# First projections in three fp32r products, and block 0 of each feed-forward in fp32, tile by tile

## The reference, cut to what matters

```python
a  = modulate(rms_norm(h, g_mix_pre), sh1, sc1)        # ac: the same of the context
y  = mixer(a, ac)                                      # layer 0: hybrid; layer 1: conformer; then: second_block's
h  = h + gt1 * rms_norm(y, g_mix_post)
f  = swiglu_ffn(modulate(rms_norm(h, g_ffn_pre), sh2, sc2), w_ffn_in, w_ffn_out)
h  = h + gt2 * rms_norm(f, g_ffn_post)
# swiglu_ffn: gate, up = split(h @ w_in); (silu(gate) * up) @ w_out      2816 hidden
# second_block's: square(relu(h @ w_ff1)) @ w_ff2                         4096 hidden
# hybrid mixer: p = a @ w_in; q, k, v of four heads = silu(conv5(p)); delta rule both ways over chunks,
#               beside it an attention of eight heads; y = concat(...) @ w_out
```

## Time and profile before

| | us |
|---|---|
| median of 3 runs | 1377.32 |
| lowest, highest | 1373.17, 1378.06 |
| profiled execution: its own time | 1380.1 |
| its span, first to last instruction | 1378.2 |
| PE busy in it | 1291.6 (94%) |
| DVE busy | 848.1 (62%) |
| ACT busy | 496.2 (36%) |

### The profile page before, as it was taken

One profiled execution on the slowest core, in us unless ns is written; L12 is line 12 of the kernel. 1 busy time (PEld: TensorE's weight loads), 2 busy tenths in 40 slices (PEclk: granted clock), 3 DMA queues, 4 the chain that ended last, 5 costly groups with the idle time before them and its releaser, 6 DMA issues. The chain is left out here.

```text
span 1378.2 us, 18690 instructions
## 1 busy us (share of the span) xinstructions
PE 1291.6 (94%) x7086; PEld 981.4 (71%) x7086; DVE 848.1 (62%) x1483; ACT 496.2 (36%) x835; POOL 119.5 (9%) x165
## 2 busy tenths in 40 slices
PE   4899979989899998999899999899999999899998
PEld 1564646544688887885388888787878886588886
DVE  1114796534777766595777777479972242677776
ACT  2243346423543334114544433311224321444443
POOL 0032021000000000200000000236530000000000
PEclk9899989999899999999999999899999999999999
DMA  9221377793555542230535455233333333455551
GB/s 392 93 100 46 130 272 277 297 369 146 216 192 192 195 173 100 101 144 2 222 145 183 183 188 190 80 109 137 138 115 114 138 107 122 140 194 184 183 184 60
DMA packets 24946, 225.75 MB, mean 164 GB/s; under 512 B 2737, under 2 KB 2865, under 8 KB 4658
## 3 DMA queue, kind: packets, MB, share of 16 engines
q1 hardware_dynamic: 23328, 220.31, 43.5%
q10 hardware_dynamic: 1554, 4.56, 0.9%
HBM read 223.81 MB, written 1.05 MB: 163 GB/s over the span
## 5 line engine op out<-in xcount | busy, mean ns | idle before, releaser
L860 PE MATMUL psum<-aT_r,arena_r 128*128 128x512 f32 x920 | 327.5, 398 | 1.4 <-DVE arena_r L2121 1.4
L777 PE MATMUL psum<-aT,ring 128*128 128x256 f32 (+1 forms) x1216 | 302.7, 407 | 1.5 <-DVE aT L2078 1.5
L2121 DVE TENSOR_TENSOR arena_r<-ring,arena_r 128x1024 fp32r<-128x1024 f32 x193 | 225.9, 1220 | 112.4 <-ACT arena_r L1556 112.4
L777 PEld LDWEIGHTS psum<-aT,ring 128*128 128x128 f32 x1216 | 231.0, 192 | 66.7 <-issue 38.7
L861 PE MATMUL psum<-aT_r,arena_r 128*128 128x256 f32 x920 | 258.2, 281 | 0.0
L1556 ACT ACTIVATE arena_r<-ring 128x1024 fp32r<-128x1024 f32 x193 | 191.6, 1051 | 149.6 <-PE psum L901 132.5
L901 PE MATMUL psum<-arena_r 128*128 128x512 f32 x876 | 213.5, 392 | 0.0
L860 PEld LDWEIGHTS psum<-aT_r,arena_r 128*128 128x128 f32 x920 | 172.8, 188 | 43.8 <-issue 1.9
L901 PEld LDWEIGHTS psum<-arena_r 128*128 128x128 f32 x876 | 159.5, 188 | 34.8
L861 PEld LDWEIGHTS psum<-aT_r,arena_r 128*128 128x128 f32 x920 | 173.7, 189 | 2.6
L1568 ACT ACTIVATE nrm<-nrm 128x256 f32<-128x256 f32 x76 | 31.8, 418 | 171.3 <-DVE nrm L2135 171.3
(11 more groups left out here) (442 smaller groups left out, 1479.7 us busy)
## 6 DMA issues: line engine op xcount, KB each, us to landing
ring<-in_w_ffn SPq DMA_DIRECT2D x44, 1536.0 KB, 6.5
ring<-in_w_mod SPq DMA_DIRECT2D x32, 1536.0 KB, 9.2
ring<-in_w_ff SPq DMA_DIRECT2D x32, 1024.0 KB, 4.9
ring<-in_w_in_g SPq DMA_DIRECT2D x8, 1536.0 KB, 6.4
ring<-in_w_conf_i SPq DMA_DIRECT2D x8, 1024.0 KB, 4.9
ring<-in_w_hyb_f SPq DMA_DIRECT2D x4, 1536.0 KB, 6.4
ring<-in_w_in_a SPq DMA_DIRECT2D x4, 1536.0 KB, 6.3
ring<-in_w_in_b SPq DMA_DIRECT2D x4, 1536.0 KB, 6.5
```

What stands on the lines that cost most here:

```text
L777: last = mm(bank(use)[:, out_at:out_at + rhs(k).shape[1]], weights[:, k * P:(k + 1) * P], rhs(k), start=(k == 0), stop=(k == KT - 1))
L860: mm(bank(use).rearrange("p (a t) -> p a t", a=2), hi, x_both[:, :, k, :], start=(k == 0), stop=False)
L2121: tt(lo, slot(c)[:, at], hi.bitcast(F32), ALU.subtract).then_inc(split_ready, 1)
```

## The change

**First projections.** `hyb_tokens(1)`, `(2)` and feature blocks 0 to 4 run in fp32r parts. The transposed activations get a hi and a lo (four pairs of k each, `a_hi`, `a_lo`), and so do the weights, in eleven parts (`HYB_PARTS`: three of each token chunk, one for each block). ACT writes the hi of a part into one of three buffers, DVE the lo over the weights in the ring. Each fp32 product becomes three fp32r products. Token chunks 3 and 0 and feature blocks 5 to 11 stay fp32. The convolution of the key goes block by block, with the silu of each behind it.

**Feed-forward, block 0.** It multiplies the fp32 weights in the ring with fp32 `yT`, one tile of 128 tokens at a time, into banks 4 and 5 (free once tile 0 of the output is read). Tile 0 is transposed inside the output's products of tile 1 (before their last two), and its block is computed behind them; then tile 1's transposes and block. x_hi and x_lo are made behind tile 1's evacuation. `split` of chunk 0 keeps only its output part; ahead of `row_diag` the splits of chunk 1's first parts are put in ffn0 (two parts) and ff (one), while ffn1 leaves these where they were, inside `ffn`. SP waits for block 0's product before the load of chunk 4.

```diff
+HYB_PARTS = [("hyb_t", _c, _k * HYB_TC, _n * HYB_TC) for _c in (1, 2) for _k, _n in ((0, 3), (3, 3), (6, 2))]
+HYB_PARTS += [("hyb_f", _b // 3, _b % 3 * D, D) for _b in range(5)]
-USE["norm2"] = BANKS.turn(4, (2, 0, 3, 1))
-USE["ffn0"], USE["ffn0_up"] = BANKS.turn(NF, (0, 1)), BANKS.turn(NF, (2, 3))
+USE["norm2"] = BANKS.turn(8, (2, 3, 0, 1))
+USE["ffn0"] = [BANKS.take(4)] + BANKS.turn(NF - 1, (1, 0))
+USE["ffn0_up"] = [BANKS.take(5)] + BANKS.turn(NF - 1, (3, 2))
...
 # SP
+                if name in FFNS:
+                    wait_full(sp, USE["ff" if name == "ff" else name + "_up"][0])
...
 # PE
+            def norm_tile(i, t):
+                for kp in range(4):
+                    use = USE[f"norm{i}"][4 * t + kp]
+                    pe.wait_ge(norm_x, 4 * i + 2 * t + kp // 2 + 1)
+                    wait_free(pe, use)
+                    for j in range(2):
+                        k = 2 * kp + j
+                        last = nc.tensor.transpose(bank(use)[:, j * P:(j + 1) * P], nrm[:, t, k * P:(k + 1) * P], ident)
+                    filled(last, use)
...
                             last = rows_of(c, kk, t)
+                            if t and c == 3 and kk == 0:
+                                norm_tile(p + 2, 0)
...
+                def first_block(t):
+                    if t == 0:
+                        wait_ring(c0)
+                        pe.wait_ge(y_gained, 4 * (p - 1) + 2)
+                        pe.wait_ge(post_ss, 4 * (p - 1) + 2)
+                    else:
+                        wait_part(0, parts - 1, 0)
...
+                        for k in range(KT):
+                            if part == 0 and k % 2 == 0:
+                                wait_read(pe, USE[f"norm{norm_i}"][4 * t + k // 2])
+                            at = part * D + k * P
+                            last = mm(bank(use)[:, t * P:(t + 1) * P], slot(c0)[:, at:at + P], yT[:, k, t * P:(t + 1) * P],
+                                      start=(k == 0), stop=(k == KT - 1))
...
-                block_first()
+                first_block(0)
+                norm_tile(norm_i, 1)
+                first_block(1)
+                pe.wait_ge(x_own, 2 * norm_n + 2)
+                pe.wait_ge(x_rounded, 2 * norm_n + 2)
+                pe.wait_ge(x_split, 4 * norm_n + 4)
                 block_in(1)
+                wait_y(p)
                 block_out(0)
...
+            def tokens_in_parts(c):
...
+                for k in range(KT):
+                    n, at = 3 * (c - 1) + k // 3, k % 3 * HYB_TC
+                    if k % 3 == 0:
+                        pe.wait_ge(hyb_lo, 4 + n + 1)
...
+                        for x, y in ((x_h, hi), (x_h, lo), (x_l, hi)):
+                            last = mm(bank(use)[:, 0:HYB_TC], x, y, start=(k == 0 and x is x_h and y is hi),
...
+            def features_in_parts(blocks):
+                for b in blocks:
+                    n, use = 6 + b, USE["hyb_f"][b]
+                    wait_free(pe, use)
+                    pe.wait_ge(hyb_lo, 4 + n + 1)
...
+                        for x, y in ((x_h, hi), (x_l, hi), (x_h, lo)):
+                            last = mm(bank(use), y, x, start=(k == 0 and x is x_h and y is hi), stop=(k == KT - 1 and y is lo))
...
-            hyb_features(0, (1, 2))
-            hyb_features(1, (3, 4))
+            features_in_parts((1, 2, 3, 4))
...
 # ACT
+            def part_high(n):
+                name, c, _, width = HYB_PARTS[n]
+                act.wait_ge(ring_ready[SLOT_OF[CHUNK[name, c]]], 16 * (TURN_OF[CHUNK[name, c]] + 1))
...
+                fn(part_hi[n % 3][:, 0:width], part_of(n, ring), ACT.Copy).then_inc(hyb_hi, 1)
             act.wait_ge(margins, 1)
+            for kp in range(4):
+                for i in range(2):
+                    wait_read(act, USE[f"norm{i}"][kp])
+                fn(a_hi[kp], aT[:, 2 * kp:2 * kp + 2, :], ACT.Copy).then_inc(hyb_hi, 1)
+            act.wait_ge(mod_taken, 1)
+            for n in range(3):
+                part_high(n)
             tokens_evac(3)
...
+            for n in (3, 4, 5):
+                part_high(n)
             tokens_evac(1)
+            for n in (6, 7, 8):
+                part_high(n)
             tokens_evac(2)
...
-            split("ffn0", 0, range(3))
+            split("ffn0", 0, [2])
+            split("ffn0", 1, [0, 1])
             for t in range(TT):
                 post_stats(0, (t,))
                 if t == 0:
                     row_copy(1)
                 norm_stats(2, (t,))
-            act.wait_ge(mod_ready, 2)
-            norm_evac(2)
+                act.wait_ge(mod_ready, 2)
+                tile_evac(2, t)
+            x_round(2)
...
 # DVE
+            def part_low(n):
+                dve.wait_ge(hyb_hi, 4 + n + 1)
+                width = HYB_PARTS[n][3]
+                tt(part_of(n, ring_r), part_of(n, ring), part_hi[n % 3][:, 0:width].bitcast(F32), ALU.subtract).then_inc(hyb_lo, 1)
...
-            conv5((0, 1))
-            conv5((2, 3))
-            conv5((4,))
+            conv5((0,))
+            part_low(10)
+            for b in range(1, 5):
+                conv5((b,))
...
-            split("ffn0", 0, range(3))
+            split("ffn0", 0, [2])
+            split("ffn0", 1, [0, 1])
             row_diag(1)
             for t in range(TT):
                 post(0, (t,))
                 norm_scale(2, (t,))
-            norm_evac(2)
+                tile_evac(2, t)
+            x_parts(2)
```

More of the change, by code:

```diff
@@ L284, with splits @@
 USE["row", 5] = BANKS.turn(2, (2, 3))
-USE["norm6"] = BANKS.turn(4)
-USE["ff"] = BANKS.turn(NF2, (0, 1))
+USE["norm6"] = BANKS.turn(8)
+USE["ff"] = [BANKS.take(4)] + BANKS.turn(NF2 - 1, (1, 0))
 take_y(("y", 5))
 AGAIN = SLOTS // 2
-FFNS = {"ffn0": (3, 0, 0), "ffn1": (3, 3 * NF, NF - 1), "ff": (2, 6 * NF, 2 * NF - 2)}
+FFNS = {"ffn0": (3, 0, 0), "ffn1": (3, 3 * NF - 2, NF - 1), "ff": (2, 6 * NF - 4, 2 * NF - 2)}
+def splits(name, j, part):
+    parts, before, _ = FFNS[name]
+    return before + parts * j + part + 2 - parts
 DONE = []
@@ L843, in ffn @@
                 uses = [USE[name], USE[name + "_up"]] if parts == 3 else [USE[name]]
[L844 removed]
+                c0, norm_i = FIRST[name], p + 1
                 def wait_part(j, part, i):
[L847 removed]
+                    pe.wait_ge(split_ready, splits(name, j, part) + SLOTS * parts * i)
                 def block_in(j, i=0):
@@ L1510, in norm_evac, with tile_evac, x_round @@
                     freed(last, use)
+            def tile_evac(i, t):
+                for kp in (1, 3):
+                    use = USE[f"norm{i}"][4 * t + kp]
+                    wait_full(act, use)
+                    for j in range(2):
+                        k = 2 * kp + j
+                        last = fn(yT[:, k, t * P:(t + 1) * P], bank(use)[:, j * P:(j + 1) * P], ACT.Identity,
+                                  scale=ngain[:, i, k:k + 1], bias=nshift[:, i, k:k + 1])
+                    freed(last, use)
+            def x_round(i):
+                for kp in (1, 3):
+                    for t in range(TT):
+                        wait_read(act, USE[f"norm{i}"][4 * t + kp])
+                    fn(x_hi[:, 2 * kp:2 * kp + 2, :], yT[:, 2 * kp:2 * kp + 2, :], ACT.Copy).then_inc(x_rounded, 1)
             def row_copy(p):
@@ L1890, in _ @@
             act.wait_ge(bbar_ready, 1)
-            split("ffn1", 0, range(3))
+            split("ffn1", 0, [2])
             for t in range(TT):
@@ L1984, in _ @@
             act.wait_ge(merged, 8)
-            split("ff", 0, range(2))
+            split("ff", 0, [1])
+            split("ff", 1, [0])
             for t in range(TT):
@@ L2116, in split @@
                 for part in todo:
-                    dve.wait_ge(split_hi, before + parts * j + part + 1 + SLOTS * parts * i)
+                    dve.wait_ge(split_hi, splits(name, j, part) + SLOTS * parts * i)
                     at = slice(part * D, part * D + D)
@@ L2195, in _ @@
             ts(g_t, g_t, -1.0, None, ALU.mult).then_inc(g_ready, 1)
+            for n in range(3, 6):
+                part_low(n)
             use = USE["gates"]
@@ L2201, in _ @@
             last.then_inc(dsum, 1)
+            for n in range(6, 9):
+                part_low(n)
             dve.wait_ge(att_sq_ready, 4)
```

192 lines of the change are left out of this document (110 added, 82 removed).

## The result

The changed kernel takes 1367.83 us (median of 8 runs, 1361.53 to 1370.88) against 1376.42 us (8 runs, 1373.17 to 1378.06) for the kernel before, run beside it: ratio 0.9935, 95% interval 0.9922 to 0.9947. That is 8.6 us faster; the forecast was 6.9 us. The profiled execution took 1368.44 us, its span is 1366.7 us, 11.5 us shorter than the one of before.

The account below looks back on a forecast made before the run. TensorE, busy 94% of a 1378.2 us span, was taken as the bound. Stage 1 -10.1 and the three sites +4.2, -2.9, +1.9 sum to -6.9 us: 1371.3 in span, 1370.4 as a median; range 1361 to 1378.

Parts of the forecast that it names:

- the likeliest case: Whole kernel: all terms as forecast, 1370.4 us as a median, own range 1366 to 1375; chance 0.50.
- stage 1: First projections up to the keys' transposes: fp32r products and a finer key convolution save 10.1 us.
- the modulation stage: Stretch after the keys' transposes: weight loads only move along with the earlier blocks, no gain of its own.
- the first site: Output product to first feed-forward: TensorE stands 4.3 us for the diagonal, low clock after; +4.2 us.
- Second site: Output product to second feed-forward: earlier diagonal ends a 0.76 us wait; -4.2, or -2.9 with 1.3 for the clock.
- Third site: Output product to last feed-forward: load lands near 1170.6, diagonal wait 1.4 us, low clock 1.6; +1.9 us.
- the third decay log: First projections: it waits 0.7 us for the gates' bank, as ScalarE copies part 8 before emptying it.
- Parts come late: Rival, first projections: parts arrive only when TensorE stands before them, half of 10.1 stays; -1.8, 1375.5 us; chance 0.20.
- T: Start of tile 1's transposes at each site; block 1 was to start at T+5.3, at the last T+5.1.

Follow-up runs that it names:

- the two pairs of traces: First profiled executions of the kernel before and the changed kernel, then second traces of both, unchanged: repeats measured 1376.11 and 1365.52 us.
- projections only: Kernel before with only the first projections in fp32r parts and the key's convolution block by block; feed-forwards as before: 1364.02 us, ratio 0.9915.
- filled or not: Filled: kernel before with 32 unread identity transposes in each of TensorE's three waits before tile 1's transposes, 1372.32 us; not filled: kernel before, unchanged.
- feed-forwards only: Kernel before with only the three feed-forwards as in the changed kernel; first projections as before: 1376.22 us, ratio 0.9998.
- features only: Changed kernel with token chunks 1 and 2 in fp32 products again, only feature blocks 0 to 4 in parts: 1365.28 us, ratio 0.9922.
- the split between the tiles: Changed kernel with the diagonal before chunk 1's split, that split between tile 0's normalisation and eviction (ffn0, ff): 1355.22 us, ratio 0.9848.
- the repeat: Kernel before, unchanged, run again for a second trace: 1376.11 us, ratio 0.9999.
- the kernel with filled waits: Apparently the split between the tiles, with 14 (ff: 28) unread identity transposes in TensorE's wait before tile 1's transposes: 1354.85 us, ratio 0.9842.

## Why the prediction was right, and where it was off

**Total.** -6.9 forecast, -8.6 measured, inside the range; the likeliest case is the one that happened, with some of its sizes wrong. That the sum is so near is partly luck: the trace is off by -0.5 in stage 1, -4.1 in the modulation stage, -0.4 at the first site, -3.0 at the second and +3.3 at the third, and the spans of the two pairs of traces differ by 11.5 and 6.7 us around a difference of medians of 8.6.

**Stage 1: -10.1 forecast; -10.6 and -9.4 in the two pairs of traces, -10.05 with the projections only.** The terms held: chunk 2 saves 8.80 - 7.18 = 1.62 (1.67), a feature block 6.87 - 5.55 = 1.32 (1.27), and the third decay log waits 0.4 for its bank (0.7). Undone by experiment, the tokens cost 2.0 to 2.4 us and the pairs of the convolution 3.2 to 3.4.

**"Parts come late"** didn't occur: no wait inside a token chunk or a feature block.

**Modulation stage: forecast 0, traces -4.1 and -2.7.** This term failed: I let the modulation weights "move along" with the keys' blocks and gave the stage no gain of its own. Their loads do begin as much earlier, but then come faster, and the stretch from the keys' transposes to the end of this stage is 1 to 4.5 us shorter with the new projections, whichever traces are compared. The projections alone gain 12.6 us by their medians, 2.5 more than their shift at 133. The late load of the first trace of before is not the reason, since the stretch is as long in two traces without it.

**First site: +4.2 forecast, +3.8.** Standstill 4.3 forecast, 4.48 and 4.47 in two traces; the low clock followed it (row product +1.9, then 6.29 instead of 5.31) and the wait of 2.18 (second half of block 0 5.26 instead of 3.8). Right in mechanism and size in the first pair; in the second the site cost +5.0.

**Second site: -2.9 forecast, -5.9 and -5.8.** Two terms. I charged 1.3 us for a fall of the clock after the wait of 2.18 us, and it stayed up: windows there show 1.00. And I took PE's own wait, 0.76 us, for all that an earlier diagonal could give. The row product comes 21.06 us after the first output product, where it came 23.3 us after it in all three traces of the kernel before, filled or not: 2.3 us, with the two splits of block 0 gone that stood ahead of the diagonal. In both unfilled traces of the kernel before the lower clock in the output products fills 1.7 us of this with busy time of PE. It cost nothing, since PE would have waited for the diagonal instead.

**Third site: +1.9 forecast, +5.2.** This is the step that failed: "its load lands near 1170.6 ... 1.4 us" took the earlier trace rows and the 4.8 us of the other loads for the load's time. In feed-forwards only, and with features only, it held (1.55 us, +1.0). In the changed kernel the load landed 2.1 us later in two of two traces; the standstill was 3.56 (+2.2), and the lower clock behind it, for which I had charged nothing, took 1.9 in the row product and 0.9 in the next twelve records (6.21 instead of 5.31). The 1.6 us that I did charge, behind T, didn't come: the products ran at the lower clock, but block 1 started at T+5.13 in both traces, at VectorE's pace.

**The clock.** The forecast read every fall as the price of the wait in front of it. Filling the wait shows that right at the third site (16 records 3.3 to 2.0 us in two of two traces). Elsewhere it is too simple: the same wait of 2.18 us before tile 1's transposes is followed by the lower clock at the first site in six of eight traces (5.2 to 5.4 us for block 0's second half) and at the second site in none (3.8), and a wait of 3.38 us before the keys' transposes was followed by none at all. The Trainium skill, TensorE: Matmul & The Clock Gate, HAM oscillation, blames waits between bursts for a next burst at the lower clock. The 0.50 behind standstills of 3.56 and 4.48 us agrees with it. Where the two waits of 2.18 us of one trace differ, and with 3.38 us at 1.00, a wait's length alone doesn't decide it.

**What the change lost** is the order of two lines: splits of a chunk whose load is under way, ahead of a diagonal that needs nothing. It ate the feed-forwards' whole gain (ratio 0.9998 alone); with the split between the tiles they are worth 1364.0 - 1355.2 = 8.8 us. Which part of them earns that (block 0 in fp32, its order tile by tile, or the splits saved) was not tried apart.

## What to carry to other kernels

When work is moved forward on an in-order engine, look at what it waits for and at everything queued behind it: a split that waits for a load must not stand ahead of a small operation for which the busy engine waits. When the bound engine gets faster, its next partner's step (here a pair of convolution blocks) becomes a wait; cut it in the same change. And before one wait of one trace is called the price of a stage, compare the whole stretch in several traces: here a single load that came 1.3 us late seemed to explain a gain that fourteen traces show with and without it.

## What the hardware showed unexpectedly

- Loads of 1024 KB of one queue, with no other load beside them, landed 4.7 to 7.4 us after their issue. The changed kernel's third site had the late one in both traces, and what came late was its last packets.
- The clock fell while PE was busy without a pause. In the first trace of before PE ran on from 639.33 (eight products there have one partition and took 3.69 us from 644.67), and the windows then show:

```profile
648.00:650.00 2.00, 2.00 (x5) 0.97 (x5) 0.53 (x2) 2.00 (x5) 0.00 (x0) 0.92 0.00 0
650.00:652.00 2.00, 2.00 (x3) 0.70 (x3) 0.17 (x1) 1.76 (x3) 0.00 (x0) 0.50 0.00 0
652.00:654.00 2.00, 2.00 (x5) 0.75 (x4) 1.70 (x12) 0.22 (x1) 0.00 (x0) 0.73 0.00 0
```

It was so in the repeat (0.50 in 646 to 648) and with projections only (0.50 in 630 to 636), and the output products of the kernel with filled waits took 22.56 us again; not in the changed kernel (1.00 throughout). It cost no time here, since the diagonal set when PE went on. Why it fell stays open.
- VectorE's four convolution steps of one block took 6.03 and 4.30 us for blocks 0 and 1 and 3.11 for the later ones, in the same trace. GpSimd is busy beside the long ones and idle beside the others (fifth busy time of each row), which points to it; it wasn't tried apart:

```profile
97.00:104.00 7.00, 7.00 (x38) 5.56 (x37) 6.35 (x5) 3.63 (x14) 6.92 (x6) 1.00 0.00 0
110.00:115.00 5.00, 5.00 (x23) 4.13 (x22) 4.86 (x6) 0.93 (x2) 1.82 (x3) 1.00 0.57 175
115.00:122.00 7.00, 7.00 (x32) 5.63 (x31) 6.44 (x10) 1.77 (x4) 0.00 (x0) 1.00 0.24 102
```
